# A quarter of the output projection computed inside the last body of the delta layer, and another order at the first step of the chain

## What is computed

```
h = rms_norm(x, norm_g[0]);  proj = h @ a_w_in          # q, k, v, gate z, two logits
q, k, v = silu(conv(q, k, v)); q, k normalised
o = gated_delta_rule(q, k, v, g, beta)                  # per head: chunks, triangular solve, then a chain over tiles
o = rms_norm(o, a_norm_g) * silu(z)                     # 2048 channels per token
x1 = x + o @ a_w_out                                    # first output projection, 2048 x 1024
h1 = rms_norm(x1, norm_g[1]);  proj = h1 @ b_w_in ...   # layer 1
```

## Time and profile before

| | us |
|---|---|
| median of 3 runs (lowest, highest) | 2341.2 (2337.7, 2341.5) |
| the profiled execution | 2340.4 |
| its span | 2338.3 |
| PE busy | 2253.6 (96%) |
| weight loads of PE | 1877.5 (80%) |
| DVE busy | 1422.8 (61%) |
| ACT busy | 1239.9 (53%) |
| GpSimd busy | 398.8 (17%) |
| mean granted clock of PE | 0.99 |

### The profile page before, as it was taken

The page is one execution under the profiler, slowest core; times in us unless marked ns, Lnnn a source line. Parts: engine busy times, 40 slices in busy tenths (PEclk is TensorE's granted clock), DMA queues, the critical chain, the costliest instruction groups (busy, mean ns, idle before and its releaser), DMA issues. The chain is left out here.

```text
span 2338.3 us, 31378 instructions
## 1 busy us (share of the span) xinstructions
PE 2253.6 (96%) x11056; PEld 1877.5 (80%) x11056; DVE 1422.8 (61%) x2602; ACT 1239.9 (53%) x2517; POOL 398.8 (17%) x672
## 2 busy tenths in 40 slices
PE   7989999999999986999999999999999999999989
PEld 6768888887878874788788888888888888888877
DVE  5756767685866763886663827457382755728341
ACT  5646566665656554556445555454545545455430
POOL 1425151533525160920000000000000000000000
PEclk9999999999999998999999999999999999999999
DMA  4122231312222222888112112111211211121151
GB/s 140 46 51 63 62 92 45 79 46 68 48 68 61 63 65 73 288 266 268 55 35 57 37 44 62 42 55 28 62 39 37 64 45 42 41 55 46 53 214 50
DMA packets 303134, 178.46 MB, mean 76 GB/s; under 512 B 97612, under 2 KB 284388, under 8 KB 302980
## 3 DMA queue, kind: packets, MB, share of 16 engines
q1 hardware_dynamic: 302980, 176.46, 26.4%
HBM read 147.85 MB, written 28.56 MB: 75 GB/s over the span
## 5 line engine op out<-in xcount | busy, mean ns | idle before, releaser
L378 PE MATMUL b_front<-g_h_hi,wb_w_hi 128*128 128x512 f32 x1280 | 507.9, 397 | 3.0 <-PEq L1397 3.0
L378 PE MATMUL b_front<-g_h_lo,wb_w_hi 128*128 128x512 f32 x1280 | 509.0, 398 | 0.0
L378 PE MATMUL b_front<-g_h_hi,wb_w_lo 128*128 128x512 f32 x1280 | 508.8, 398 | 0.0
L378 PE MATMUL a_proj<-g_h_lo,wa_w_hi 128*128 128x512 f32 x784 | 319.9, 408 | 0.0
L378 PE MATMUL a_proj<-g_h_hi,wa_w_hi 128*128 128x512 f32 x784 | 315.2, 402 | 1.4 <-PEq L245 0.9
L378 PE MATMUL a_proj<-g_h_hi,wa_w_lo 128*128 128x512 f32 x784 | 316.1, 403 | 0.0
L378 PEld LDWEIGHTS b_front<-g_h_hi,wb_w_hi 128*128 128x128 f32 x1280 | 241.2, 188 | 51.1 <-issue 3.3
L378 PEld LDWEIGHTS b_front<-g_h_hi,wb_w_lo 128*128 128x128 f32 x1280 | 241.1, 188 | 47.7
L378 PEld LDWEIGHTS b_front<-g_h_lo,wb_w_hi 128*128 128x128 f32 x1280 | 241.3, 189 | 47.0
L2035 ACT ACTIVATE b_acc<-b_front,g_gains 128x512 f32<-128x512 f32 x96 | 66.2, 690 | 301.9 <-DVE b_qk L2339 201.2
L378 PEld LDWEIGHTS a_proj<-g_h_hi,wa_w_hi 128*128 128x128 f32 x784 | 148.5, 189 | 30.6 <-issue 2.1
(11 more groups left out here) (318 smaller groups left out, 4371.6 us busy)
## 6 DMA issues: line engine op xcount, KB each, us to landing
wb_raw<-in_b_w_in_dram SPq DMA_DIRECT2D x80, 512.0 KB, 3.9
p_w_raw<-in_a_w_out_dram SPq DMA_DIRECT2D x64, 512.0 KB, 4.1
wa_raw<-in_a_w_in_dram SPq DMA_DIRECT2D x48, 512.0 KB, 4.5
a_out<-a_og SPq DMA_DIRECT2D x64, 128.0 KB, 1.9
p_a_raw<-a_out SPq DMA_DIRECT2D x64, 128.0 KB, 4.8
a_zx<-inverse_tiles SPq DMA_DIRECT2D x16, 384.0 KB, 4.5
u_tiles<-a_u SPq DMA_DIRECT2D x8, 512.0 KB, 3.2
a_bd<-u_tiles SPq DMA_DIRECT2D x32, 128.0 KB, 3.7
```

Source lines behind the costliest of these rows:

```text
L378: last = pe.matmul(out, w[:, k, :], a[:, k, ks], start=(n == 0), stop=(n == 23))
```

## The change

1. In full bodies, at the first step of the chain: DVE merges level 1 of the first pair in slot 7, behind the convolution's taps, instead of first in slot 8; DVE's weight remainder moves from slot 9 to the end of slot 8; ACT's weight split of slot 8 stands before its wait for the residual instead of behind.
2. `first` loses its own PSUM bank and lies in a part of `lev`; so the first level product of a pair waits for the merge of the pair before. `gram` lies in a bank of `front`.
3. The 16 late gate parts run two to a slot in slots 0 to 7.
4. From slot 9 of the last body on, PE makes in each slot eight of the 192 matmuls of the projection's part 0 (24 slots). SP loads 16 weight tiles, 14 of 16 token tiles of part 0 in four loads, later the rest, and the upper eight token tiles of part 1 in three loads; ACT and DVE split them. Weights and the raw tiles lie in what the last body no longer needs, the split weights in a ring of eight in the place of the layer's input `h_hi`, `h_lo`.
5. The projection block starts with the upper eight tiles of part 1, whose split weights are still in that ring (96 matmuls), then turns part 0, then runs part 1's tiles 0 to 7, and parts 2 and 3 as before. SP first loads x of part 0 and the gain, then the first group, then the positions.

```diff
-GATE_LATE = tuple(range(16))
-GATE_DONE = ((0, 30), (1, 3), (1, 9), (1, 15))
+GATE_LATE = 8
+GATE_DONE = ((0, 30), (1, 1), (1, 4), (1, 7))
+OUT_RING = 8
+OUT_TILES = A_VW // P
+OUT_TOKENS = 2 * P
+OUT_SLOT0 = GATE_LATE + 1
+OUT_WIDTH = 8
+OUT_AGAIN = 23
...
+    def products(self, pe, banks, k, order, first, last):
+
+        mm = None
+        for c in order:
+            b, n = divmod(c, 3)
+            e, half = divmod(b, 2)
+            a = self.tokens(k, n == 2, e)
+            w_ = self.weight(k, n == 1)[:, half * HALF:(half + 1) * HALF]
+            mm = pe.matmul(banks[b // 2][:, b % 2, :], a, w_, start=first and n == 0, stop=last and n == 2)
+        return mm
...
-        first = m_.ps("first", [P, 2, P])
         lev = m_.ps("lev", [P, 2, 2, P])
+        first = lev[:, :, 0, :]
         turn = m_.ps("turn", [P, HALF])
-        gram = m_.ps("gram", [P, HALF])
+        gram = front[1][:, 0, :]
...
+        def split_slot(k):
+            return OUT_SLOT0 - 1 + max(0, (3 * k - 3) // 2)
+
+        def load_slot(k):
+            return 3 + k if k < 2 else 5 if k < 4 else OUT_SLOT0 + (3 * (k - 4)) // 2
+
+        splits = sorted([(split_slot(k), 0, k) for k in range(OUT_TILES)] +
+                        [(OUT_AGAIN + (3 * i + 1) // 2, 1, OUT_RING + i) for i in range(OUT_RING)])
+        split_count = {(part, k): WEIGHTS_SPLIT + i + 1 for i, (s, part, k) in enumerate(splits)}
...
+                    if n is None:
+                        if s == 3:
+                            sp.wait_ge(og_s, H * T)
+                            sp.wait_ge(w_low, WEIGHTS_SPLIT)
+                            sp.wait_ge(o_stored, 16 * (1 + (H - 1) * T))
+                            sp.wait_ge(convs, H * 8 + 1)
+                        for k in range(OUT_TILES):
+                            if load_slot(k) == s:
+                                if k >= 4:
+                                    sp.wait_ge(w_low, split_count[0, k - 4])
+                                if k >= 2:
+                                    sp.wait_ge(w_landed[k % 2], W_LANDED[k % 2] + 16 * (k // 2))
+                                sp.dma_start(raw_weight(k), early.w[k * P:(k + 1) * P, :]).then_inc(w_landed[k % 2], 16)
+                        if s in (3, 4, 6):
+                            for k0, k1 in {3: ((0, 4),), 4: ((4, 8),), 6: ((8, 12), (12, 14))}[s]:
+                                sp.dma_start(raw_tokens(0, k0, k1), early.rows(0, k0, k1)).then_inc(o_landed, 16)
+                        if s == 11:
+                            sp.wait_ge(o_landed, 64)
+                            sp.wait_ge(ut, H * 4)
+                            sp.wait_ge(inv_out, H * (32 * PARTS_OF_BLOCK))
+                            for k0, k1 in ((8, 12), (12, 14)):
+                                sp.dma_start(raw_tokens(1, k0, k1), early.rows(1, k0, k1)).then_inc(o_landed, 16)
+                        if s in (20, 27):
+                            part = (20, 27).index(s)
+                            sp.wait_ge(o_landed, 96 + 16 * part)
+                            sp.wait_ge(o_stored, 16 * (1 + (H - 1) * T + 2 * (part + 1)))
+                            sp.dma_start(raw_tokens(part, 14, 16), early.rows(part, 14, 16)).then_inc(o_landed, 16)
...
+                            if t == 0 and n is not None:
+                                next_weight(n, s)
                             act.wait_ge(xr_mm, m * T + (t + 1))
...
+                    for at, part, k in splits if n is None else ():
+                        if at != s:
+                            continue
+                        act.wait_ge(o_landed, (64 if k < 14 else 112) if part == 0 else 112 if k < 14 else 128)
+                        act.wait_ge(proj_mm, HALVES_DONE + (k - OUT_RING + 1 if part == 0 and k >= OUT_RING else
+                                                            k + 1 if part else 0))
+                        ins = act.activation(early.tokens(k, False), raw_tokens(part, k, k + 1)
+                                             .rearrange("p k (e c) -> p (k e) c", c=P), ACT.Copy)
+                        if part:
+                            ins.then_inc(w_high, 1)
+                        else:
+                            act.wait_ge(w_landed[k % 2], W_LANDED[k % 2] + 16 * (k // 2 + 1))
+                            act.activation(early.weight(k, False), raw_weight(k), ACT.Copy).then_inc(w_high, 1)
...
+                    parts = ()
                     if is_last(n) and s in GATE_EARLY:
-                        part = GATE_EARLY.index(s)
-                    if is_last(m) and s in GATE_LATE:
-                        part = len(GATE_EARLY) + GATE_LATE.index(s)
-                    if part is not None:
+                        parts = (GATE_EARLY.index(s),)
+                    if is_last(m) and s < GATE_LATE:
+                        parts = (len(GATE_EARLY) + 2 * s, len(GATE_EARLY) + 2 * s + 1)
+                    for part in parts:
...
+                    at = (s - OUT_SLOT0) * OUT_WIDTH
+                    if n is None and 0 <= at < 12 * OUT_TILES:
+                        for k in range(at // 12, (at + OUT_WIDTH - 1) // 12 + 1):
+                            cells = range(max(at - 12 * k, 0), min(at + OUT_WIDTH - 12 * k, 12))
+                            if cells[0] == 0:
+                                pe.wait_ge(w_low, split_count[0, k])
+                                if k == 0:
+                                    pe.wait_ge(evac, HALVES_DONE)
+                                    pe.wait_ge(ut, H * 4)
+                            last = early.products(pe, front, k, cells, k == 0, k == OUT_TILES - 1)
+                            if cells[-1] == 11:
+                                last.then_inc(proj_mm, 1)
...
-                                if level:
-                                    pe.wait_ge(lv_s, m * (LEVELS * T // 2) + (use + 1))
-                                else:
+                                pe.wait_ge(lv_s, m * (LEVELS * T // 2) + (use + 1))
+                                if level == 0:
...
+                            if m is not None and s == CHAIN0:
+                                merge(m, 0, 1)
...
+                        if m is not None and s == CHAIN0 + 1:
+                            next_weight(n, s)
...
-            for part in range(PARTS):
+            load_x(0)
+            sp.dma_start(gain[:, :], norm_g[layer:layer + 1, :].partition_broadcast(P)).then_inc(gain_landed, 16)
+            load(1, 0)
+            rope_tables.load(sp)
+            load(1, 1)
+            load_x(1)
+            store(0)
+            sp.wait_ge(o_stored, 16 * (1 + H * T))
+            for part in range(2, PARTS):
                 load(part, 0)
-                if part == 0:
-                    rope_tables.load(sp)
-                    sp.dma_start(gain[:, :], norm_g[layer:layer + 1, :].partition_broadcast(P)
-                                 ).then_inc(gain_landed, 16)
                 load(part, 1)
                 load_x(part)
-                if part:
-                    store(part - 1)
+                store(part - 1)
...
+            measure(0)
+            split(1, 0)
+            keep_high(0)
+            split(1, 1)
+            for part in range(2, PARTS):
                 split(part, 0)
                 if part == 2:
                     rope_tables.take(act)
...
+            for i in range(OUT_RING):
+                early.products(pe, y[1], OUT_RING + i, range(12), i == 0, False)
+            turn(0)
+            multiply(1, 0)
+            multiply(1, 1)
+            for part in range(2, PARTS):
                 multiply(part, 0)
                 multiply(part, 1)
-                if part:
-                    turn(part - 1)
+                turn(part - 1)
```

More of the change, by code:

```diff
@@ L379, in three_passes, with __init__, weight, tokens @@
     return last
-def delta_heads(nc, g, weights, proj, o_turned):
+class EarlyProjection:
+    def __init__(self, g, weights, w, o_turned):
+        self.g, self.weights, self.w, self.o_turned = g, weights, w, o_turned
+    def weight(self, k, low):
+        return (self.g.h_lo if low else self.g.h_hi)[:, k % OUT_RING, :]
+    def tokens(self, k, low, e=None):
+        r = k % OUT_RING
+        tile = (self.weights.lo if low else self.weights.hi)[r // 4]
+        at = 2 * (r % 4)
+        return tile[:, at:at + 2, :] if e is None else tile[:, at + e, :]
+    def products(self, pe, banks, k, order, first, last):
[7 more added lines that the diff above has]
+        return mm
+    def rows(self, part, k0, k1):
+        cols = slice(part * OUT_TOKENS, (part + 1) * OUT_TOKENS)
+        return self.o_turned[k0 * P:k1 * P, cols].rearrange("(k p) n -> p k n", p=P)
+def delta_heads(nc, g, weights, proj, o_turned, front, o_stored, early):
     with ExitStack() as ctx:
@@ L1071, in body @@
                         b, k = divmod(s - LEVEL0 - 2, LEVEL_STEP)
[L1072 to L1083, removed]
```

(29 more changed lines are left out.)

129 lines of the change are left out of this document (85 added, 44 removed).

## The result

The changed kernel takes 2355.4 us (median of 4 runs, 2354.9 to 2357.2), the kernel before 2340.6 us in the runs beside it. The ratio is 1.0070, with a 95% interval of 1.0056 to 1.0084: slower, by 15 us. Predicted were 2357.5 us and 2345 to 2371.

The account below looks back on a forecast made before the run. PE was taken to set the time, except where something is late. The second group of part 2 moved from 1040.0 to 1056.3, +16.3 us on 2341.2, about 2357.5 us; range 2345 to 2371 us.

Parts of the forecast that it names:

- Part 1: Chain's first step in seven bodies: the residual's DVE merge comes 0.94 us earlier, 6.6 us in all, bounds 0 and 11.5.
- Part 2: Gates two to a slot, last body: 4.5 us of added matmuls fill nearly the whole 4.72 us wait for inverse tiles.
- Part 3, the start: Early quarter in the last body: loads in by 883, first early matmul at 886.4, some 7 us of PE idle.
- Part 3, the chain waits: Seven chain steps of the last body: PE waits of 2 us in all, between 0 and 13.4 us.
- Two of the signs: Right: about 7 us of gap before the first early matmul; wrong: a last body over 105 us long on PE.
- The hand-over: From the last body to the projection block: 2.1 us left of 3.5, bounds 1.2 and 3.5.
- X: First issue of the projection block, forecast at 954.5 us; before the change 924.15.
- Part 4: Projection block: ACT waits for GpSimd's 72.8 us rope-table chain; PE idles 43 us and resumes at X + 99.4.
- The end: Behind the second group of part 2, 16.3 us late, both kernels run the same PE-bound order; 2357.5 us in all.
- The rival of the short table chain: Projection block: GpSimd's chain shrinks from 72.8 to about 31 us, about 2312 us; 7 in 100.
- The rival of a chain-bound last body: Last body: each step keeps its 1.92 us and loads are 3 us later, about 2372 us; 10 in 100.
- The rule of the Trainium skill that was weighed there: Projection block: DVE with two SBUF inputs and GpSimd lock each other out, so the chain is shorter while DVE idles.

Follow-up runs that it names:

- e1: The changed kernel with ACT taking the rope tables in part 3 of the projection instead of part 2: 2318.3 us, ratio 0.9912.
- e2: The kernel before with only DVE's and ACT's new order at the chain's first step, no early quarter, no shared bank: 2331.5 us, ratio 0.9968.
- e7: e6 with DVE making the remainders of all early tiles but the first two one slot later: 2304.0 us, ratio 0.9845.
- e6: e1 with the early quarter's first loads sooner and the first four tiles' splits waiting only for their own token load: 2311.1 us, ratio 0.9881.
- e5: The kernel before with the rope tables taken in part 1 of the projection instead of part 2: 2362.1 us, ratio 1.0097.

## Why the prediction was right, point by point

The forecast came true by its own mechanism: the gain in the last body came, and was lost in the next block to ACT's wait for GpSimd. Both halves were shown by taking the wait away in the changed kernel and by bringing it about in the old one. The terms of the sum:

- **Part 1**, 6.6 us: 6.6 us of gap measured with that part alone, 7.6 us of time (0.2 to 0.4% by the interval). The bodies came out 104.17 us long instead of 105.11, which is the 0.94 us of the argument. In the changed kernel the seven gaps together lost 8.2 us: the first fell from 3.09 to 0.46 us, where the part alone brought it to 2.14. No run here shows what took the other 1.7 us off.
- **Part 2**, the wait for the inverse tiles down to 0.2 us: 0.40 us, and the clock stayed at its upper level there (1.00 between 859 and 869 us).
- **Part 3, the start**: the first early matmul was forecast at 886.4 - 6.6 = 879.8 and came at 882.8. The rows of the changed kernel, SP, ACT and PE:

```profile
860.12 0.54 SPq L704 DMA_DIRECT2D a_out<-a_og  x1
...
865.14 0.35 SPq L685 DMA_DIRECT2D wa_raw<-in_a_w_out_dram  x1
...
879.79 0.42 ACT L925 ACTIVATE wa_w_hi<-a_attn 128x256 fp32r<-128x256 f32 x1 [8.65 <-DMA a_x_raw<-a_out]
...
882.80 0.79 PE L418 MATMUL b_front<-g_h_hi,wa_w_hi 128*128 128x512 f32 x1 [10.97 <-DVE g_h_lo L1354]
```

Two terms were sized too small. The landing of head 6's last store: 2 us was taken from its issue to the first load, from the median of all stores, and 5.0 us measured, 4.3 of them SP's wait. The store is issued right behind 1 MB of reads of the inverse tiles; that these delay it is likely and was not tried. And the loads: the text has 881.5 to 886 us for their end, but its own 3.9 MB at 0.27 and 0.24 MB/us give 883.9 and 885.8, so 883 lay under both. Measured were 14.65 us from the first load to the first split, 0.27 MB/us. The hand-over took the 3.0 us of the earlier trace rows.
- **Part 3, the chain waits**: 2 us taken, 4.1 measured in four waits (0.2, 1.1, 1.4 and 1.4 us). The argument was that eight matmuls (1.8 us) cover each wait, as in the full bodies. It overlooked that DVE may itself stand in a wait for ACT's split: the cover has to hold against what is queued ahead on DVE, not against its busy time. The stretch from the first early matmul to PE's last turning took 75.5 us instead of 72.6.
- **Two of the signs**: the gap ahead of the first early matmul was named as about 7 us and was 11.0. And "a last body over 105 us long on PE" was named as a sign of being wrong; the last body runs on PE from 851.74 to 958.3, that is 106.6 us, so this sign appeared. The sum had 99.8 us. Of the 6.8 us more, 3.9 lie ahead of the first early matmul (3.0 for its lateness, 0.8 because PE entered the body sooner than forecast) and 2.9 behind it. They were made good elsewhere, as the last points show, so the time was right while this part of the sum was not.
- **The hand-over**: 2.1 us taken, 1.3 measured (from PE's last turning, which ends at 958.3, to 959.59). So X was 959.6 instead of 954.5, 5.1 us late.
- **Part 4**: GpSimd started at X + 15.8, forecast was 11.7 + 4.2 = 15.9. Its chain took 69.5 us, not 72.8: while DVE stands still some of its instructions are shorter. ACT's table load (1.28 us) ran ahead of the wait, where the sum had it behind. PE resumed at X + 94.7 instead of X + 99.4. These 4.7 us offset the 5.1 us of X: both were errors, of opposite sign, and the close agreement at that point (1054.3 forecast as 1053.9 without the clock's 2.4 us) owes something to luck.
- **The end**: the third turning came 17.2 us later than before (1113.37 to 1096.19 in the earlier trace rows), 0.9 more than forecast, while the spans differ by 14.9 only. The 2.3 us between lie behind the projection; a lower clock that one of the two profiled executions has at the start of the attention accounts for 1.7 us of them (last section).

The rival of the short table chain falls: the chain lost 3.3 us, where some 40 were needed. One argument against it did not hold, though: "most instructions stand within 0.01 us of 2.83, which no interference would give". Of the 25 there are 8, and with DVE idle the same forms took 2.76 us. The rival of a chain-bound last body was true in kind, four waits of 0.2 to 1.4 us, 4.1 of the 13.4 us that it had for them. The rule of the Trainium skill that was weighed there (SBUF — State Buffer, "SBUF: two separate sides") agrees with the trace as far as it goes: in the changed kernel an instruction of GpSimd with two inputs took 2.33 us with DVE idle and 2.99 to 3.40 with DVE at work, and DVE's token remainder, 0.41 us at its shortest, up to 2.49 us beside GpSimd. But most of the GpSimd instructions with one tensor as input went from 2.83 to 2.76 us only, and the whole chain was less than 5% shorter. What the Trainium skill holds of interleaving regimes (Perfetto Trace Analysis, "Optimization Strategy") agrees with e1 and e2: 13.2 us were there to be had, once the cover of the rope tables was kept.

## What to carry to other kernels

When work is moved out of a stage, every wait that stood behind it in that stage moves up with it: go through each engine's order there, and compare the time from the stage's start to each wait with the time that its releaser takes from the same start. An in-order engine that waits for a side product (tables, needed only in the next stage) should do so as late as the next stage allows. And a filler between the steps of a latency-bound chain should stand behind the chain's next instruction on every engine that it passes, not only on the one that it is meant to fill: here moving it on DVE alone removed all four waits (e7).

## What the runs showed of the hardware

The projection block ends in all nine kernels with the same 3.0 us of idle PE ahead of the attention. In seven of the profiled executions the clock of the next 10 us was 0.83 or 0.85 of full speed, in two (the changed kernel and e6) it was 1.00, with some seven matmuls more in it. The first 10 us of attention, in the kernel before and in the changed one (columns: stretch, length, busy of PE, PEld, DVE, ACT, POOL, clock, DMA share, GB/s):

```profile
1130.14:1140.14 10.00, 10.00 (x37) 8.10 (x38) 5.44 (x13) 6.42 (x10) 0.00 (x0) 0.83 0.36 107
...
1147.32:1157.32 10.00, 10.00 (x44) 8.28 (x45) 6.99 (x15) 7.73 (x11) 0.00 (x0) 1.00 0.36 107
```

That is 1.7 us which come or stay away with one and the same work and idle time. Whether the runs of one kernel differ by it too was not measured, as each kernel has one trace. But a comparison of two single traces should look at such stretches before it explains a difference of 2 us by the change.

The other thing not expected: an ACT table load that belongs to an activation behind a wait runs ahead of that wait (1006.70 in the changed kernel, 38 us before the sine). So its 1.28 us lie within the wait when ACT is early. In e5 it was the same: the load at 979.82, the sine at 1006.45.
